# Seven products of halves for the branch projections, and GpSimd sums beside the tables of the diagonal model

## The reference, cut to what matters

```python
# first block, layers 0 and 1: gates has 3 x 1024 columns of x @ w_in
g = sigmoid(gates.reshape(B, S, 3, 1024))
merged = (g[:, :, 0] * (y_attn @ w_br_attn[l])      # 1024 -> 1024
          + g[:, :, 1] * (y_conv @ w_br_conv[l])    #  512 -> 1024
          + g[:, :, 2] * (y_mem @ w_br_mem[l]))     #  512 -> 1024
mix = merged @ w_out[l]
# second block
gates = sigmoid(proj[..., 2304:] + b_gate)          # 2 x 1024 columns of h @ w_in
mixed = (g_rwkv * (o_rwkv @ w_branch_rwkv)          #  512 -> 1024
         + g_s5 * (o_s5 @ w_branch_s5)) @ w_out     #  512 -> 1024
```

## Time and profile before

| | us |
|---|---|
| median of 3 runs | 3360.55 (3355.61 to 3363.7) |
| the profiled execution | 3368.01 |
| its span | 3366.4 |
| mean granted clock of TensorE | 0.982 |
| busy: TensorE, VectorE, ScalarE, GpSimd | 3211.0, 1470.5, 806.0, 865.2 |

### The profile page before, as it was taken

One profiled execution on the slowest core, in us unless ns is written; L12 is line 12 of the kernel. 1 busy time (PEld: TensorE's weight loads), 2 busy tenths in 40 slices (PEclk: granted clock), 3 DMA queues, 4 the chain that ended last, 5 costly groups with the idle time before them and its releaser, 6 DMA issues. The chain is left out here.

```text
span 3366.4 us, 41230 instructions
## 1 busy us (share of the span) xinstructions
PE 3211.0 (95%) x16264; PEld 2283.7 (68%) x16264; DVE 1470.5 (44%) x2641; ACT 806.0 (24%) x1780; POOL 865.2 (26%) x537
## 2 busy tenths in 40 slices
PE   8999999999999999999999899999979999999998
PEld 6857767664444687676677444447757667888886
DVE  4575512340111465746664211124487532655452
ACT  3364211121111254523330211112412211211100
POOL 4324222220000340221002200013255431353352
PEclk9999999999999999999999999999989899999999
DMA  4261121237888322022332488872200312122221
GB/s 155 100 244 51 76 75 73 78 121 295 324 327 325 149 97 87 36 103 82 113 125 105 186 321 325 324 294 116 97 31 31 116 61 100 51 75 100 76 100 50
DMA packets 54212, 470.87 MB, mean 140 GB/s; under 512 B 5888, under 2 KB 10368, under 8 KB 30592
## 3 DMA queue, kind: packets, MB, share of 16 engines
q1 hardware_dynamic: 29040, 379.00, 30.2%
q0 software_dynamic: 21136, 78.39, 5.9%
q10 hardware_dynamic: 3840, 10.75, 0.9%
HBM read 506.65 MB, written 63.18 MB: 169 GB/s over the span
## 5 line engine op out<-in xcount | busy, mean ns | idle before, releaser
L665 PE MATMUL bank<-B,ring 128*128 128x256 f32 x4080 | 900.2, 380 | 15.5 <-PEq L1434 4.4
L665 PEld LDWEIGHTS bank<-B,ring 128*128 128x128 f32 x4080 | 775.7, 191 | 133.0 <-issue 25.5
L649 POOL TENSOR_TENSOR ring<-ring 128x1024 f32<-128x1024 f32 x58 | 149.7, 2581 | 1183.1 <-DMA ring<-in_w_static 376.4
L2098 PE MATMUL bank<-ring,B 128*128 128x512 f32 x960 | 419.1, 594 | 0.6 <-issue 0.6
L815 ACT ACTIVATE B<-bank 128x256 f32<-128x256 f32 x384 | 145.4, 384 | 1026.3 <-PE bank L665 1024.0
L665 PE MATMUL bank<-XT,ring 128*128 128x256 f32 x1472 | 339.8, 385 | 22.8 <-DMA ring<-in_w_static 9.8
L665 PEld LDWEIGHTS bank<-XT,ring 128*128 128x128 f32 x1472 | 283.7, 193 | 70.0 <-issue 21.3
L2098 PEld LDWEIGHTS bank<-ring,B 128*128 128x128 f32 x960 | 180.2, 190 | 219.1 <-issue 218.6
L553 PE MATMUL bank<-B,ring 128*128 128x512 f32 x672 | 291.6, 592 | 3.5 <-DVE B L1499 3.5
L2173 DVE TENSOR_TENSOR B<-B,bank 128x512 f32<-128x512 f32 x46 | 31.6, 688 | 467.4 <-PE bank L2098 407.1
L553 PEld LDWEIGHTS bank<-B,ring 128*128 128x128 f32 x672 | 127.5, 190 | 157.6 <-issue 156.7
(11 more groups left out here) (533 smaller groups left out, 4014.4 us busy)
## 6 DMA issues: line engine op xcount, KB each, us to landing
ring<-in_w_expert SPq DMA_DIRECT2D x96, 2048.0 KB, 8.8
ring<-in_w_static SPq DMA_DIRECT2D x78, 2048.0 KB, 7.6
B<-in_w_expert SPq DMA_DIRECT2D x42, 2048.0 KB
slots_y<-B POOLq DMA_DIRECT2D x52, 512.0 KB, 27.5
B<-slots_x POOLq DMA_DIRECT2D x44, 512.0 KB
slots_x<-B POOLq DMA_DIRECT2D x23, 512.0 KB, 16.2
ring<-s_tables SPq DMA_DIRECT2D x4, 2048.0 KB, 8.2
s_tables<-tmp POOLq DMA_DIRECT2D x8, 512.0 KB, 3.0
```

The costliest lines, as they stand in the source:

```text
L649: pool.tensor_tensor(s(0), w(1, 0), w(1, 1), ALU.add).then_inc(made.up(), 1)
L665: ins = pe.matmul(out, left, right, start=start and k == 0, stop=k == 3, skip_group_check=not start)
L2098: ins = pe.matmul(bank[:, :], xbT[q % 2][:, k, :], slot[:, k, :], start=k == 0, stop=k == KT - 1)
```

## The change

All five branch projections are made by seven products too. An attention half (512 of 1024 outputs from 1024 inputs) is a chunk of full size. Of the other branches, with 512 inputs, each half of the outputs is a "part": products of two k-tiles instead of four, token and weight sums of 128 x 512, two parts sharing one load of weights and one slot of sums. The results go to SBUF and are multiplied with the gates from there, a group of four tiles at a time (`merge_group`), instead of one by one from the banks. The order of chunks changes, the ring has a slot of sums for every branch weight, and no slot is kept aside. In layer 1 GpSimd makes all weight sums; VectorE makes the tables' steps at new places.

```diff
-EARLY_BRANCH = {("in", _l, 14): ("br_mem", _l, 0) for _l in range(DEPTH)}
+BRANCHES = ("br_attn", "br_conv", "br_mem", "br_rwkv", "br_s5")
...
-    return name[0] in SPLIT or name[0] == "ffn_down" or name[0] == "in2" and name[2] != 4
+    return name[0] in SPLIT or name[0] in BRANCHES or name[0] == "ffn_down" or name[0] == "in2" and name[2] != 4
...
+    names += [("in", l, 10), ("br_attn", l, 0), ("in", l, 11), ("br_attn", l, 1), ("in", l, 12), ("br_conv", l, 0)]
+    names += [("in", l, 13), ("in", l, 14), ("in", l, 15), ("br_mem", l, 0)]
...
 class SevenProducts:
+    def tiles(self, n):
+        return 4 if self.parts[n] is None else 2
...
+TURNS_BESIDE_CHUNK = {2: (0, 1), 3: (2, 3), 4: (4, 5), 5: (6,), 6: (7,), 7: (8, 9, 10), 8: (11, 12, 13), 9: (14, 15)}
+LAST_COSINES = 10
+COSINES_BESIDE_CHUNK = {3: (0, 1), 4: (2, 3), 5: (4,), 6: (5,), 7: (6, 7, 8), 8: (9, 10, 11), 9: (12, 13), 10: (14, 15)}
...
 def merge(m, l):
+    order = [("gate", 0), ("value", 0), ("gate", 1), ("value", 1), ("gate", 2), ("value", 2), ("value", 3), ("gate", 3),
+             ("gate", 4), ("gate", 5), ("value", 4), ("value", 5)]
+    before = {("gate", 1): 0, ("gate", 2): 1, ("value", 2): None, ("gate", 3): 2, ("gate", 4): 2, ("gate", 5): 3}
...
         @block.scalar
+            for n, (kind, g) in enumerate(order):
+                used = before.get((kind, g))
+                if used is not None:
+                    act.wait_ge(*m.tally("scaled_tiles").at(4 * used + 2))
+                seven.keep_first(act, n, copy_to(dest(n)))
+                if used is not None:
+                    act.wait_ge(*m.tally("scaled_tiles").at(4 * used + 4))
+                seven.keep_fifth(act, n, copy_to(dest(n)))
+                if tables and n == 1:
+                    tables.first_angles(act)
+                seven.keep_sixth(act, n, copy_to(dest(n)))
+                if tables and n == 0:
                     tables.steps(act)
+                if ready:
+                    sigmoids(ready.pop())
+                if tables and n in TURNS_BESIDE_CHUNK:
+                    for s in TURNS_BESIDE_CHUNK[n]:
                         tables.sines(act, s)
+                seven.last_quarter(act, n, copy_to(dest(n)))
+                if kind == "gate":
+                    ready.append(g)
...
         @block.vector
+            def merge_group(g):
+                dve.wait_ge(*m.tally("gates").at(4 * g + 4))
+                for c in range(4):
+                    value, j = value_of[g][:, c, :], 4 * (g % 2) + c
+                    seven.finished(dve, at["value", g], c // 2, c % 2)
+                    if g < 2:
+                        dve.tensor_tensor(value, value, gate_of[g][:, c, :], ALU.mult).then_inc(scaled_tiles.up(), 1)
+                        continue
+                    dve.tensor_tensor(value, value, gate_of[g][:, c, :], ALU.mult).then_inc(m.tally("dve_step").up(), 1)
+                    dve.wait_ge(*m.tally("dve_step").last())
+                    dve.tensor_tensor(merged[:, j, :], merged[:, j, :], value, ALU.add).then_inc(scaled_tiles.up(), 1)
+
             seven.sum_tokens(dve)
+            for n, (kind, g) in enumerate(order):
+                if (kind, g) == ("gate", 2):
+                    seven.sum_tokens(dve, n=at["value", 2], unused=bk.made(seven.key("x", at["value", 1], 1)))
+                if (kind, g) == ("gate", 3):
+                    seven.sum_tokens(dve, n=at["value", 4], unused=bk.made(seven.key("x", at["value", 3], 1)))
+                if tables and (kind, g) == ("value", 0):
+                    tables.angles(dve)
+                    tables.constants(dve)
+                if tables and n in TURNS_BESIDE_CHUNK:
+                    for s in TURNS_BESIDE_CHUNK[n]:
+                        if s >= 2:
+                            tables.cosines(dve, s - 2)
+                        tables.turns(dve, s)
+                if tables and n == LAST_COSINES:
+                    tables.cosines(dve, 14)
+                    tables.cosines(dve, 15)
+                seven.add_sums(dve, n, dest(n))
+                if n == 0:
+                    seven.sum_tokens(dve, n=at["value", 0])
+                if kind == "value" and g != 3:
+                    merge_group(g)
+                if (kind, g) == ("gate", 4):
+                    merge_group(3)
...
         @block.gpsimd
             seven.sum_weights(pool, 0)
+            seven.sum_weights(pool, 1)
             pool.wait_ge(*m.tally("s5_matrix").at(1))
             pool.dma_start(m.dram["s5_scaled_c"], tables.cnew).then_inc(m.matrix_stored, 16)
+            for n in range(1, len(order)):
+                for s in COSINES_BESIDE_CHUNK.get(n, ()):
+                    pool.wait_ge(*m.tally("s5_cosines").at(s + 1))
+                    pool.dma_start(m.dram["s5_tables"][s // 4, :, (s % 4) * 1024:(s % 4 + 1) * 1024], tables.pair[s % 2]).then_inc(m.tables_stored[s % 2], 16)
+                if n + 1 < len(order):
+                    seven.sum_weights(pool, n + 1)
...
 def second_merge(m):
+    order = [("gate", 0), ("value", 0), ("value", 1), ("gate", 1), ("gate", 2), ("gate", 3), ("value", 2), ("value", 3)]
```

More of the change, by code:

```diff
@@ L1433, in merge @@
-    place = within(lambda c: sig[:, c, :])
-    with m.stage() as block:
[L1435 to L1438, removed]
+    beside = m.memT[:, :, :].rearrange("p (a b) t -> p a (b t)", b=2) if tables else m.tmp[:, :, :]
+    attn = attended, blocks(sig[:, 4:8, :], beside), 1
+    conv = m.B[2][:, 0:4, :], column_quarters(attended[:, 4:8, :]), 2
+    mem = m.B[2][:, 4:8, :], column_quarters(attended[:, 4:8, :]), 3
@@ new lines, in merge, with dest @@
+    before = {("gate", 1): 0, ("gate", 2): 1, ("value", 2): None, ("gate", 3): 2, ("gate", 4): 2, ("gate", 5): 3}
+    with m.stage() as block:
+        for kind, g in order:
+            if kind == "gate":
+                seven.chunk(("in", l, 10 + g))
+            elif g < 2:
+                seven.chunk(("br_attn", l, g), inputs=attn)
+            else:
+                seven.chunk((("br_conv", "br_mem")[g // 2 - 1], l, 0), part=g % 2, inputs=(conv, mem)[g // 2 - 1])
+        def dest(n):
+            kind, g = order[n]
+            return within(lambda c: (gate_of if kind == "gate" else value_of)[g][:, c, :])
@@ L1440, in _ @@
         @block.tensor
         def _(pe):
-            for n in range(6):
+            for n in range(len(order)):
                 seven.multiply(pe, n)
[L1444 to L1456, removed]
@@ L1458, in _, with sigmoids @@
         @block.scalar
         def _(act):
[L1460 to L1468, removed]
-                for c in (2, 3, 0, 1):
-                    seven.finished(act, n, c // 2, c % 2)
-                    act.activation(sig[:, c, :], sig[:, c, :], ACT.Sigmoid).then_inc(m.tally("gates").up(), 1)
+            def sigmoids(g):
+                for c in (2, 3, 0, 1):
+                    seven.finished(act, at["gate", g], c // 2, c % 2)
+                    act.activation(gate_of[g][:, c, :], gate_of[g][:, c, :], ACT.Sigmoid).then_inc(m.tally("gates").up(), 1)
@@ L3327, in _ @@
         def _(dve):
[L3328 to L3343 removed]
+            scaled_tiles = m.tally("scaled_tiles")
```

228 lines of the change are left out of this document (105 added, 123 removed).

## The result

The changed kernel takes **3372.86 us**, the median of 20 runs (3366.6 to 3379.21); the kernel before, beside it, 3360.84 (20 runs, 3355.61 to 3366.0). The ratio is **1.0035**, 95% interval 1.0028 to 1.0042: 12.0 us slower, inside the forecast range of 3350 to 3402, but 14.7 us short of the +26.7 that was forecast.

The account below looks back on a forecast made before the run. TensorE was taken as the bound, its matrix row busy 95% of the span. Terms -33.0 - 4.3 + 9.2 + 8.7 + 3.0 + 32.6 + 10.5 gave +26.7 us on 3360.55, so 3387.3 us; range 3350 to 3402.

Parts of the forecast that it names:

- products, ten units: Four attention halves and six other branches on TensorE, each 24.17 us instead of 27.47: 33.0 us less.
- the three ends, waiting: At each merge's end TensorE waits for the last part's four tiles to be scaled and added: 9.2 us more.
- the three ends, clock: Slower TensorE clock behind the longer wait at each merge's end, 2.9 us three times: 8.7 us more.
- waits in layer 0 and second merge: Fourth product waits a little where an extra part's merge meets other work: 3.0 us more, bounds 0 and 7.
- waits in layer 1: Chunks late in gate 1, value 3, gate 3 and gate 4 of layer 1's merge: 32.6 us more.
- clock in layer 1: Slower clock behind layer 1's four waits, three at 2.9 us and the first at 1.8: 10.5 us more.
- GpSimd beside the tables: Layer 1: each GpSimd sum delays a VectorE instruction working in SBUF alone by 2.05 us; with clock 43.1 us more.
- the clock's price: TensorE's loss behind long waits: 2.9 us at each end and after three layer 1 waits, 1.8 after gate 1.
- Rival 2: The waits come but the clock stays: +7.5 us, 3368 us; chance 0.17.
- Rival 1: VectorE and GpSimd pass each other in layer 1, so the kernel ends faster: 3340 to 3349 us; chance 0.13.
- rival 3: Late chunks push GpSimd's sums onward, gate 5 and value 4 wait too: 8 to 13 us more; chance 0.12.
- Rival 4: A part's small last product runs slower if its first bank is copied late: +4 us, no chance of its own.

Follow-up runs that it names:

- e6: Changed kernel with 18 throw-away matmuls on TensorE behind each of the three merges; 3368.66 us, ratio 1.0018 to the kernel before.
- e9: Kernel before, with GpSimd instead of VectorE making layer 1's weight sums and direct projections kept; 3375.91 us against 3362.53, ratio 1.0035.
- e5: Changed kernel with throw-away matmuls filling layer 1's four waits (gate 1, value 3, gate 3, gate 4); 3363.75 us, ratio 1.0007 to the kernel before.
- e4: Changed kernel with each angle cut to one VectorE instruction, seven of its eight left out; 3334.73 us (one run).
- e2: Changed kernel with GpSimd's layer 1 sums, from the second chunk on, covering only 4 of 256 columns; 3342.5 us (one run).
- e3: Changed kernel with GpSimd making the next chunk's layer 1 weight sums before it waits for the cosines, not after; 3376.27 us (one run).
- e1: Changed kernel with VectorE making layer 1's weight sums again from the third chunk on; 3345.31 us against 3363.62 for the kernel before, ratio 0.9947.
- e7: e1 with two angles and several cosines of layer 1 moved one chunk later; 3342.45 us, ratio 0.9941 to the kernel before.
- e8: e7 plus e6's throw-away matmuls behind the three merges; 3337.11 us, ratio 0.9925 to the kernel before.

## Why the forecast had the right sign and the wrong size

The terms as forecast, and as the stages and runs show them:

| term | forecast | measured | from |
|---|---|---|---|
| products, ten units | -33.0 | -33.0 | pace held, also in parts |
| old gaps of layer 1 | -4.3 | -4.3 | gone |
| the three ends, waiting | +9.2 | +7.1 | 4.6 instead of 2.2 us |
| the three ends, clock | +8.7 | +4.5 | e6 |
| slow stretches that before has itself | 0 | -3.4 | e9 against before |
| waits in layer 0 and second merge | +3.0 | +2.6 | 1.03 + 1.55 |
| waits in layer 1 | +32.6 | +29.1 | five rows |
| clock in layer 1 | +10.5 | +7.0 | e5 |
| not assigned | | +1.4 | |
| sum | +26.7 | +11.0 | stages |

**Right: the mechanism and its place.** The part "GpSimd beside the tables" held step by step: gate 1 waited 3.07 us (forecast 4), value 3 7.59 (9.0), gate 3 6.49 (7.6), gate 4 11.41 (12.0), and gates 2 and 5 not at all. The price of 2.05 us a sum held (13.2 - 4.7 over four sums is 2.1), and adds from banks were untouched: all 136 of the corner add took 0.41 to 0.43 us. Layer 1's merge is 36.3 us longer than layer 0's, where 41 were forecast. The lock of the Trainium skill's page SBUF — State Buffer, section "SBUF: two separate sides", is thus seen in kind, but at 2.05 to 2.1 us a sum and not at the full 2.35 of GpSimd's instruction. e4 and e2 show that neither half makes the waits alone. That the cosine's signal "makes the collision certain" is shown for gate 4 only: there the collision went when the sums no longer followed the signal (e3). In gate 3 it came without the signal too.

**The step that failed: the clock's price.** The prediction took 2.9 us for a wait of 5 us or more, three times at the ends and three times in layer 1, from one place where 16 matmuls took 6.53 us, and "no loss" for short gaps. Against e5 and e6 the four waits of layer 1 cost 7.0 us and the three ends 4.5. With 19.2 us forecast and 11.5 measured, that is 7.7 of the 15.7 us of error.

The price has no fixed size. From 17 waits of 2.6 us or more inside layer 1's merge, in six executions (changed kernel, e1, e2, e3, e6, e9), the matmuls behind one lose 1.5 to 3.1 us by the pace, 2.2 on average. So 2.9 is near the top of what occurs, and was taken for six of seven waits; the prediction's other row, 1.8 us behind a wait of 2.83, is as typical. At the ends the step also missed an overlap: a part of the slow stretch only fills a wait for VectorE's token sum that would come at full clock (e6). Measured against e6, the three ends cost 2.9 to 6.2 us in the seven executions of the new order that have them unfilled, never 8.7.

Another 3.4 are the same step's other half: before pays already. Its gap of 2.21 us ahead of the stage behind the second merge is followed by 23.29 us for 99 matmuls, where the pace makes 21.4; 1.9 us of slow clock stood in a row that I had quoted and did not divide. The same code in e9, whose second block is that of before, has no such loss. TensorE's timeline of before:

```profile
2701.13 26.10 PE L665 MATMUL bank<-B,ring 128*128 128x256 f32 x112 [1.90 <-PEq L2431]
...
2856.89 50.27 PE L665 MATMUL bank<-B,ring 128*128 128x256 f32 x224 [2.21 <-PEq L3288]
```

and of e9:

```profile
2713.28 24.41 PE L665 MATMUL bank<-B,ring 128*128 128x256 f32 x112 [1.90 <-PEq L2432]
...
2867.35 48.58 PE L665 MATMUL bank<-B,ring 128*128 128x256 f32 x224 [2.21 <-PEq L3289]
```

Twice 1.69 us behind the same waits. e9 in turn pays 0.6 us behind each of its first two merges, where before pays nothing (51.55 and 51.49 against 50.92). How often an execution of before pays was not measured, so these 3.4 us belong to its profiled execution, 7.2 us above the median, and only in part to the median.

**Mis-sized, each by a little.** The late chunks were put 0.6 to 1.4 us too late, 4.0 in all; one wait of 0.55 us for ScalarE in value 3 was not foreseen. The ends wait 4.6 us and not 5.3, since four multiplies and adds in a row take 5.4 us (639.38 to 644.77 in layer 0) and not 8 x 0.72 = 5.8: an instruction that doesn't need the one before starts ahead of its end. The same explains a part of the late chunks' difference: in value 3 the merge of group 2 took 5.3 us (1656.76 to 1662.07) and not 5.8.

**The rivals.** Rival 2 (the waits come, the clock stays, +7.5) was half true: the clock was lost, but at some 60% of the price (11.5 of 19.2 us). Rival 1 (the engines pass each other) was refuted by four waits, rival 3 (a chain into gate 5 and value 4) by their absence. Rival 4 left no row in layer 0. In layer 1 a wait of 0.55 us for ScalarE's copy of the part before stands at the start of value 3 (1.78 in e1, 2.02 in e7), where its sines stand ahead of that copy.

**Still open.** The 1.55 us of the second merge are one collision as well: GpSimd's sum begins when its weights land (2743.93, in VectorE's list of sums of squares). In e4 to e8 that wait did not occur: in e5, e6 and e8 the stage is 1.8 us shorter, in e4 and e7 a slow stretch at its start costs as much instead. I did not try to steer it. Nor was the share of these differences in a median measured.

## What to carry to other kernels

Moving work from VectorE to GpSimd does not free VectorE while both work in SBUF: here a sum of 128 x 1024 cost VectorE 1.2 us when it made it itself and 2.1 when GpSimd did, so the helper pays only in stretches where VectorE is idle or reads banks. Whether it helps depends on when: in layer 0, with the same sums on GpSimd and no tables, the only wait inside the merge is 1.03 us. A change of two parts should be priced and run as two: one was worth -18 us, the other cost more than that. Before a clock loss is charged to new waits, divide the rows behind the old waits by the pace, since the old kernel may already pay, and in more than one execution, since the loss behind the same wait varies.

## What the runs showed of the hardware that I had not expected

- The same wait is followed by a slow stretch in one execution and by none in another. Behind the 1.90 us ahead of the second merge, before, e4 and e7 lose 1.7 us and the other eight executions nothing. The Trainium skill, in TensorE: Matmul & The Clock Gate, Part 1, calls the number of slow matmuls at a kernel's start run-variable; these rows show the same in the middle of a kernel.
- The loss behind a wait does not follow its length: 1.7 us after 3.07 and 1.8 after 11.41 in one execution, 2.9 after 3.08 in another (e6), 1.5 and 3.1 after two waits of 5.06 in e9. Filling the waits with small matmuls left less than 0.1 us at each of the four places (e5, by the pace), though TensorE then went on to wait 0.9 to 1.4 us for VectorE there.
- A VectorE instruction with a single SBUF tensor input (L1396, L1402) is held up just like one with two: 3.07 and 2.45 us instead of 0.43. GpSimd is slowed too, from 2.35 to 2.78 us.
